# Depthwise convolution in a buffer of its own, with its taps behind each value group, its gate product read from PSUM, and the pooled maps between input chunks

## What is computed

```
mod = silu(c) @ w_ada + b_ada                    # six parts: sh1, sc1, g1, sh2, sc2, g2
h   = rmsnorm(x, norm1) * (1 + sc1) + sh1
u, gate_b, gate_c, val = split(h @ w_in)         # four times 512 columns
pooled = mean over the last 2/4/8/16 rows of u, minus u    # one window per group of 128 channels
A   = (pooled @ w_pool, per group) * pool_scale
v   = gate_c * val
B   = gate_b * (w0 * v[t-2] + w1 * v[t-1] + w2 * v[t])     # depthwise convolution, three taps
x   = x + g1 * (concat[A, B] @ w_out)
h2  = rmsnorm(x, norm2) * (1 + sc2) + sh2
x   = x + g2 * moe(h2)                           # router, top 4 of 32 experts, clamped SwiGLU
y   = rmsnorm(x, final_norm)
```

## Time and profile before

| | |
|---|---|
| median of 3 executions | 1440.04 us (1436.89 to 1440.72) |
| the profiled execution | 1436.63 us, span 1434.8 us from first to last instruction |
| granted TensorE clock, mean | 0.954 of full speed |
| busy in the span: TensorE | 1278.8 us, 89% |
| VectorE, GpSimd, ScalarE | 459.5, 282.2, 135.3 us |
| DMA | 479.23 MB, mean 334 GB/s |

### The profile page before, as it was taken

The page is one execution under the profiler, slowest core; times in us unless marked ns, Lnnn a source line. Parts: engine busy times, 40 slices in busy tenths (PEclk is TensorE's granted clock), DMA queues, the critical chain, the costliest instruction groups (busy, mean ns, idle before and its releaser), DMA issues. The chain is left out here.

```text
span 1434.8 us, 32026 instructions
## 1 busy us (share of the span) xinstructions
PE 1278.8 (89%) x13745; PEld 746.7 (52%) x13745; DVE 459.5 (32%) x676; ACT 135.3 (9%) x270; POOL 282.2 (20%) x335
## 2 busy tenths in 40 slices
PE   4999989566999999999999999999999999999710
PEld 2777634311356556655555665544545666566500
DVE  1210153452222333322223333222233333222244
ACT  3100101200000000100000000100000001000102
POOL 4002100152111111222111111221111112220126
PEclk9999989779999999999999999999999999999955
DMA  9736830625999999999999999999999999999161
GB/s 325 223 111 230 329 145 30 257 101 198 398 417 409 412 413 410 409 398 395 419 416 411 405 412 410 406 406 416 409 412 408 411 407 396 414 405 415 44 260 68
DMA packets 88787, 479.23 MB, mean 334 GB/s; under 512 B 15235, under 2 KB 24939, under 8 KB 39061
## 3 DMA queue, kind: packets, MB, share of 16 engines
q1 hardware_dynamic: 73842, 456.59, 79.5%
q0 software_dynamic: 11840, 20.64, 4.1%
q10 hardware_dynamic: 3075, 1.58, 0.5%
HBM read 468.41 MB, written 17.84 MB: 339 GB/s over the span
## 5 line engine op out<-in xcount | busy, mean ns | idle before, releaser
L1433 PE MATMUL acc<-raw_b,ht 128*32 128x512 f32 x3120 | 376.2, 597 | 16.2 <-DVE ht L1264 9.0
L1433 PE MATMUL acc<-raw,ht 128*32 128x512 f32 x3024 | 371.6, 596 | 12.5 <-DVE ht L1264 6.5
L1433 PEld LDWEIGHTS acc<-raw,ht 128*32 128x32 f32 x3024 | 168.7, 110 | 185.2 <-issue 155.4
L1433 PEld LDWEIGHTS acc<-raw_b,ht 128*32 128x32 f32 x3120 | 146.2, 110 | 220.7 <-issue 204.2
L1154 POOL DMA_INDIRECT rows<-h_rows,row_next x90 | 91.6, 1018 | 752.2 <-DVE row_next L1259 732.8
L1312 DVE TENSOR_TENSOR g_sb<-acc,bias_gu 128x768 f32<-128x768 f32 x32 | 30.7, 958 | 623.7 <-PE acc L1433 623.7
L1451 PE MATMUL acc<-raw,at 128*32 128x256 f32 x3168 | 198.2, 379 | 2.7 <-DVE at L1270 2.6
L1451 PE MATMUL acc<-raw_b,at 128*32 128x256 f32 x2976 | 186.9, 379 | 0.0
L1451 PEld LDWEIGHTS acc<-raw,at 128*32 128x32 f32 x3168 | 144.2, 109 | 37.1 <-DVE at L1270 3.1
L1451 PEld LDWEIGHTS acc<-raw_b,at 128*32 128x32 f32 x2976 | 138.2, 110 | 41.2 <-issue 8.3
L909 PE MATMUL acc<-h_t,raw 128*128 128x288 f32 (+1 forms) x512 | 118.4, 393 | 1.1 <-DVE h_t L670 1.1
(11 more groups left out here) (217 smaller groups left out, 546.1 us busy)
## 6 DMA issues: line engine op xcount, KB each, us to landing
raw<-in_w_down SPq DMA_DIRECT2D x66, 1024.0 KB, 9.0
raw_b<-in_w_gate SPq DMA_DIRECT2D x65, 1024.0 KB
raw_b<-in_w_up SPq DMA_DIRECT2D x65, 1024.0 KB
raw<-in_w_gate SPq DMA_DIRECT2D x63, 1024.0 KB, 7.0
raw<-in_w_up SPq DMA_DIRECT2D x63, 1024.0 KB, 9.3
raw_b<-in_w_down SPq DMA_DIRECT2D x62, 1024.0 KB
raw<-in_w_ada SPq DMA_DIRECT2D x24, 1024.0 KB, 11.7
raw<-in_w_in SPq DMA_DIRECT2D x8, 1024.0 KB, 13.8
```

The source lines that it names most:

```text
L1433: mm = pe.matmul(gu_ps[b][q * TB:(q + 1) * TB, :].rearrange("p (m n) -> p m n", m=2), ht[:, b, k, :], w[:, kk, :, q * CW:(q + 1) * CW], st ...
```

## The change

The convolution's result gets a tile of its own in `ring_b`, behind `g1_bc`, so that `mix_t` becomes a list of eight views: four in `h_t`, four in `conv`. The three taps of a group, prompt and sample, follow the value product of that group. The gate_b groups are not copied out by ScalarE: VectorE multiplies `conv` by them straight from PSUM, and TensorE waits for these products before it reuses the buffer. The sample's pooled windows move ahead of these products, the addition of SC2 behind the second, that of G2 behind the fourth. Three pooled maps run between `ada(SC2)` and `project(7)`, the fourth after `ada(G2)`, in other PSUM banks than before; ScalarE writes them to `h_t` once the last projection is done. On SP's queue, store(3) goes ahead of expert loads 2 to 5, and these wait for the last mix as well. "..." marks what is left out.

```diff
@@ -139,7 +139,6 @@
         junk = sb("junk", [P, D])
         h_row = [sb(f"h_row{i}", [P, D]) for i in range(2)]
         h_t = sb("h_t", [P, KT, NTOK])
-        mix_t = h_t
...
         pooled = done_first([GR, NTOK])
-        conv = h_t[:, GR:2 * GR, :]
...
         vext = done_first([GR, CPAST + SEQ])
         vext_s = done_first([GR, DEC_B, CPAST + DEC_T])
         g1_bc = done_first([D])
+
+        conv = done_first([GR, NTOK])
...
+        mix_t = [h_t[:, g, :] for g in range(GR)] + [conv[:, g, :] for g in range(GR)]
...
-        pm_p = [acc_g[:, 0, :], acc_g[:, 1, :], acc_u[:, 0, :], acc_u[:, 1, :]]
+        pm_p = [tp[:, 0, :], tp[:, 1, :], acc_y[:, 1, :], tp[:, 0, :]]
         mixp = [acc_g, acc_u]
...
@@ -355,10 +356,11 @@
                 store(t)
             sp.wait_ge(tp_full, TP["so0"] + 1)
             sp.wait_ge(new_packed, 4)
+            store(3)
             sp.wait_ge(x1_ready, PT)
+            sp.wait_ge(mix_done, TT)
             for n in range(2, SLOTS):
                 first(n)
-            store(3)
             for n in range(XSLOTS - OUT_CH, XSLOTS):
                 sp.wait_ge(*used(DENSE_CH - XSLOTS + n))
                 first(n)
...
@@ -563,17 +565,15 @@
                 leave(GR + g, gate_c[:, g, 0:SEQ], by_seq(gate_c[:, g, SEQ:NTOK]))
-            leave(3 * GR, gate_b[:, 0, 0:SEQ], by_seq(gate_b[:, 0, SEQ:NTOK]))
-            leave(3 * GR + 1, gate_b[:, 1, 0:SEQ], by_seq(gate_b[:, 1, SEQ:NTOK]))
-            leave(3 * GR + 2, gate_b[:, 2, 0:SEQ], by_seq(gate_b[:, 2, SEQ:NTOK]))
-            leave(3 * GR + 3, gate_b[:, 3, 0:SEQ], by_seq(gate_b[:, 3, SEQ:NTOK]))
 
             for g in range(GR):
                 act.wait_ge(pm_done, g + 1)
-                act.activation(mix_t[:, g, 0:SEQ], pm_p[g], ACT.Identity, scale=par[:, g:g + 1]).then_inc(pm_ready, 1)
+                if g == 0:
+                    act.wait_ge(z_done, 4 * GR)
+                act.activation(mix_t[g][:, 0:SEQ], pm_p[g], ACT.Identity, scale=par[:, g:g + 1]).then_inc(pm_ready, 1)
             act.wait_ge(tp_full, TP["pm_s"] + 1)
             for g in range(GR):
-                act.activation(mix_t[:, g, SEQ:NTOK], tp[:, 0, g * NS:(g + 1) * NS], ACT.Identity,
+                act.activation(mix_t[g][:, SEQ:NTOK], tp[:, 0, g * NS:(g + 1) * NS], ACT.Identity,
                                scale=par[:, g:g + 1]).then_inc(pm_ready, 1)
...
+            def by_seq(t_):
+                return t_.rearrange("p (s t) -> p s t", t=DEC_T)
+
+            def taps(v, y, g):
+
+                n = y.shape[-1]
+                tap = [par[:, (1 + j) * GR + g:(1 + j) * GR + g + 1] for j in range(3)]
+                step(dve.tensor_scalar(y, v[..., 0:n], tap[0], None, ALU.mult))
+                step(dve.scalar_tensor_tensor(out=y, in0=v[..., 1:1 + n], scalar=tap[1], in1=y,
+                                              op0=ALU.mult, op1=ALU.add))
+                step(dve.scalar_tensor_tensor(out=y, in0=v[..., 2:2 + n], scalar=tap[2], in1=y,
+                                              op0=ALU.mult, op1=ALU.add))
+
             add_ada(G1)
             for g in range(GR):
 
@@ -715,29 +728,11 @@
                 dve.tensor_tensor(vext_s[:, g, :, CPAST:CPAST + DEC_T], z_sample[f % 2],
                                   gate_c[:, g, SEQ:NTOK].rearrange("p (s t) -> p s t", t=DEC_T), ALU.mult)\
                     .then_inc(v_s_ready, 1)
+                dve.wait_ge(v_ready, g + 1)
+                dve.wait_ge(v_s_ready, g + 1)
+                taps(vext[:, g, :], conv[:, g, 0:SEQ], g)
+                taps(vext_s[:, g, :, :], by_seq(conv[:, g, SEQ:NTOK]), g)
             add_ada(SH2)
-            add_ada(SC2)
-            dve.wait_ge(n2_loaded, 16 * Q)
-            scale_rows(SC2, n2_rows)
-
-            def taps(v, y, b, g, ready):
-
-                n = y.shape[-1]
-                tap = [par[:, (1 + j) * GR + g:(1 + j) * GR + g + 1] for j in range(3)]
-                step(dve.tensor_scalar(y, v[..., 0:n], tap[0], None, ALU.mult))
-                step(dve.scalar_tensor_tensor(out=y, in0=v[..., 1:1 + n], scalar=tap[1], in1=y,
-                                              op0=ALU.mult, op1=ALU.add))
-                step(dve.scalar_tensor_tensor(out=y, in0=v[..., 2:2 + n], scalar=tap[2], in1=y,
-                                              op0=ALU.mult, op1=ALU.add))
-                if b is not None:
-                    dve.tensor_tensor(y, y, b, ALU.mult).then_inc(ready, 1)
-
-            add_ada(G2)
-            dve.wait_ge(z_done, 4 * GR)
-            dve.wait_ge(v_ready, GR)
-            for g in range(GR):
-                dve.wait_ge(z_evac, 2 * (2 * GR + g + 1))
-                taps(vext[:, g, :], conv[:, g, 0:SEQ], gate_b[:, g, 0:SEQ], g, conv_ready)
             bufs = [b[:, 0:DEC_B * (PAST + DEC_T)].rearrange("p (s r) -> p s r", s=DEC_B) for b in wsum]
             for g, w in enumerate(WINDOWS):
...
@@ -746,13 +741,18 @@
                                          in1=uext_s[:, g, :, PAST:PAST + DEC_T],
                                          op0=ALU.mult, op1=ALU.subtract).then_inc(pooled_s_ready, 1)
                 dve.wait_ge(pooled_s_ready, g + 1)
-            dve.wait_ge(v_s_ready, GR)
-
-            def by_seq(t_):
-                return t_.rearrange("p (s t) -> p s t", t=DEC_T)
-
             for g in range(GR):
-                taps(vext_s[:, g, :, :], by_seq(conv[:, g, SEQ:NTOK]), by_seq(gate_b[:, g, SEQ:NTOK]), g, conv_s_ready)
+                f = 3 * GR + g
+                dve.wait_ge(z_done, f + 1)
+                v = conv[:, g, 0:SEQ].rearrange("p (b n) -> p b n", b=2)
+                dve.tensor_tensor(v, v, z_prompt[f % 2], ALU.mult).then_inc(conv_ready, 1)
+                v = by_seq(conv[:, g, SEQ:NTOK])
+                dve.tensor_tensor(v, v, z_sample[f % 2], ALU.mult).then_inc(conv_s_ready, 1)
+                if g == 1:
+                    add_ada(SC2)
+                    dve.wait_ge(n2_loaded, 16 * Q)
+                    scale_rows(SC2, n2_rows)
+            add_ada(G2)
 
...
@@ -898,8 +898,11 @@
                     if 2 * GR + 2 <= f < 3 * GR + 2:
                         pe.wait_ge(v_ready, f - 2 * GR - 1)
                         pe.wait_ge(v_s_ready, f - 2 * GR - 1)
+                    elif f >= 3 * GR + 2:
+                        pe.wait_ge(conv_ready, f - 3 * GR - 1)
+                        pe.wait_ge(conv_s_ready, f - 3 * GR - 1)
                     elif f >= 2:
-                        pe.wait_ge(z_evac, 2 * (f - 1 if f < 2 * GR + 2 else f - 1 - GR))
+                        pe.wait_ge(z_evac, 2 * (f - 1))
...
             ada(SH2)
             project(6)
             ada(SC2)
+            pe.wait_ge(small_loaded, 16 * 3)
+            pe.wait_ge(pooled_ready, GR)
+
+            def pool_map(g):
+                pe.matmul(pm_p[g], wpool_sb[:, g, :], pooled[:, g, 0:SEQ], start=True, stop=True).then_inc(pm_done, 1)
+
+            for g in range(GR - 1):
+                pool_map(g)
             project(7)
             ada(G2)
-
-            pe.wait_ge(small_loaded, 16 * 3)
-            pe.wait_ge(pooled_ready, GR)
-            for g in range(GR):
-                pe.wait_ge(z_evac, 2 * (3 * GR - 1 + g // 2))
-                pe.matmul(pm_p[g], wpool_sb[:, g, :], pooled[:, g, 0:SEQ], start=True, stop=True).then_inc(pm_done, 1)
+            pe.wait_ge(pm_ready, 1)
+            pool_map(GR - 1)
 
             def mix(t):
 
                 r, out_ = norm_rows(t), mixp[t % 2]
                 if t >= 2:
                     pe.wait_ge(x1_ready, t - 1)
+                if t == 1:
+                    pe.wait_ge(conv_s_ready, GR)
                 for j in list(range(GR, 2 * GR)) + list(range(GR)):
                     w = chunk("out", j // KC)
+                    if t == 0 and j >= GR:
+                        pe.wait_ge(conv_ready, j - GR + 1 if j < 2 * GR - 2 else GR)
+                    if t == 0 and j < GR:
+                        pe.wait_ge(pm_ready, j + 1)
                     if t == PT:
                         for q in range(Q):
-                            mm = pe.matmul(out_[q * NS:(q + 1) * NS, 0, 0:QW], mix_t[:, j, SEQ:NTOK],
+                            mm = pe.matmul(out_[q * NS:(q + 1) * NS, 0, 0:QW], mix_t[j][:, SEQ:NTOK],
                                            w[:, j % KC, q * QW:(q + 1) * QW], start=(j == GR), stop=(j == GR - 1))
                         continue
                     for h in range(2):
-                        mm = pe.matmul(out_[0:r, h, :], mix_t[:, j, t * P:t * P + r],
+                        mm = pe.matmul(out_[0:r, h, :], mix_t[j][:, t * P:t * P + r],
                                        w[:, j % KC, h * HALF:(h + 1) * HALF], start=(j == GR), stop=(j == GR - 1))
                 mm.then_inc(mix_done, 1)
...
-            pe.wait_ge(pm_ready, GR)
-            pe.wait_ge(conv_ready, GR)
+
+            pe.wait_ge(conv_ready, GR - 1)
+            pe.wait_ge(conv_s_ready, GR - 1)
             mix(0)
             take("pm_s")
```

## The result

The changed kernel took 1431.28 us (median of 10 runs, 1425.69 to 1434.27), the kernel before 1439.23 us (10 runs, 1435.52 to 1443.10). The ratio is 0.9944, 95% interval 0.9927 to 0.9961: 8.1 us faster, between 5.6 and 10.5. The profiled execution took 1431.78 us with a span of 1429.7 us, 5.1 us less than before.

A forecast was written before the change was run, and what follows sets the result against it. The first block's end was taken to hang on store(4), queued behind expert loads. Mixing stage -10.2 us plus queue +5.5 gave -4.7, from 1440.0 to 1435.3 us; the range was 1429 to 1439.5.

The forecast's parts named there:

- The hole and the clock: Ahead of mix(0): closing TensorE's hole gains 7.8 us, and mix(0) without the clock drop 2.4, together 10.2 us.
- Taps, windows, gate products, maps at cost 0: Projections: moved taps and windows fit VectorE's idle time, PSUM gate products take equally long, moved maps keep TensorE's sum; cost 0.
- w_out chunks (rival C): Before mix(0): w_out chunks land late and stall it; net +2.9 us (1443) to +9.1 us (1449), chance 0.04.
- store(4) behind the loads, and the block's end behind store(4): End of first block: store(4) lands after the expert loads queued ahead, at 286.3, and the second block waits for it.
- rival A: End of first block: loads do not carry the end; gain up to 11.9 us, time 1428 to 1430, chance 0.10.
- queue term: SP's queue: it starts with store(3) at 264.69 instead of loads at 259.16, so its end shifts 5.5 us later.
- The sum: Whole kernel: -10.2 us from the mixing stage plus 5.5 from the queue gives -4.7 us, time 1435.3 us.
- the rivals: Block end free of loads, chance 0.10; new small wait and clock dip, 1438 to 1441, 0.12; late w_out chunks, 0.04.
- Faster by over 0.3%: Whole kernel: gain of more than 4.3 us; given 0.54 for faster, against 0.42 same and 0.04 slower.
- The dip of the clock: Later mixes: mix(2) took 15.68 instead of 13.98 us; without that dip the gain is 6.4, with one more 3.0.

The follow-up runs named there:

- convolution part alone: The changed kernel with conv in the tile gate_b instead of the ring and SP's queue as before the change: ratio 0.9923 to the kernel before, 10.7 us faster.
- late maps: The changed kernel with all four pooled maps after ada(G2), as before the change: ratio 0.9960 to the kernel before, 5.5 us faster.
- copied gate: The changed kernel with gate_b copied out by ScalarE and the product reading the SBUF copy: ratio 0.9955 to the kernel before, 6.5 us faster.
- queue part alone: The kernel before with only store(3) ahead of loads 2 to 5 and these waiting for the last mix: ratio 1.0037, 5.1 us slower.
- store(3) behind: The changed kernel with loads 2 to 5 ahead of store(3) again, both waits kept: ratio 0.9952 to the kernel before, 6.7 us faster.
- the repetition: The whole change, unedited, run again against the kernel before on the chip where that takes 1437.8 us: ratio 0.9940, 8.6 us faster.

## Why the prediction was right, point by point

- **The hole and the clock: 10.2 us.** Right: 10.37 in the profile, 10.7 (9.0 to 12.5) by the convolution part alone.
- **Taps, windows, gate products, maps at cost 0.** Right, each with cover left: 3 us behind the taps, 2.9 behind the windows, 3.7 between the last gate product and mix(0). The late maps and the copied gate, each undone alone, leave project(6) to mix(0) at 40.45 us. All of the gain comes from the taps' new place; of the parts in the change's title, the gate product from PSUM and the moved maps are worth nothing as long as the rest is there (both undone together wasn't run).
- **w_out chunks (rival C).** mix(0) runs 13.9 us without a gap; the late three landed in 4.7, 6.5 and 9.3 us. The last, issued at 177.68, was there at 187.0, and mix(0) comes to it at 187.11 + 3.5 = 190.6.
- **store(4) behind the loads, and the block's end behind store(4).** Right, and shown from both sides: the queue part alone costs time, and taking the store away from behind the loads brings time in both kernels. In all eight profiles in which it was queued behind them, store(4) landed 0.2 to 0.4 us after the last load (before 0.4, after 0.2, with store(3) behind 0.3). The prediction set this against the Trainium skill (DMA: Bandwidth & Descriptors, Queues, rings and completion order), by which completions need not come in order. It had read half of the rule: the same section says that the increment that reports a transfer lands only after every earlier write of the same DMA engine, so store(4) can't report ahead of loads on engines that it shares with them. With that half the rule agrees with the traces and gives rival A no ground. One reading of the prediction was slightly off: TensorE was 3.3 us ahead of store(4)'s landing (286.3 - 283.03), and the 3.9 are to the second block's start.
- **The size of the queue term** is the step that was off: "its end shifts by 264.69 - 259.16 = 5.5 us". It shifted by 3.2 (after), 3.4 (the repetition) and 3.6 (queue part alone). The same bytes needed 27.1 us from the queue's first issue to store(4)'s landing before, 24.9 after. I had taken that stretch as fixed, on the ground that the DMA engines were full in it. Rows of one microsecond show where it went:

Stretches (columns as in rows 1), the kernel before:

```profile
260.00:261.00 1.00, 1.00 (x24) 0.60 (x20) 0.00 (x0) 0.83 (x2) 0.47 (x1) 1.00 0.76 156
282.00:283.00 1.00, 0.69 (x20) 0.61 (x20) 0.20 (x1) 0.00 (x0) 0.00 (x0) 0.50 0.95 387
283.00:284.00 1.00, 0.03 (x2) 0.00 (x0) 0.00 (x0) 0.00 (x0) 0.00 (x0) 0.50 0.27 107
284.00:285.00 1.00, 0.00 (x0) 0.00 (x0) 0.00 (x0) 0.00 (x0) 0.00 (x0) 0.50 0.10 41
```

Stretches (columns as in rows 1), the changed kernel:

```profile
257.00:258.00 1.00, 0.58 (x6) 0.34 (x4) 0.86 (x4) 0.38 (x1) 0.00 (x0) 1.00 0.73 295
278.00:279.00 1.00, 0.00 (x0) 0.00 (x0) 0.00 (x0) 0.00 (x0) 0.00 (x0) 0.50 0.99 418
279.00:280.00 1.00, 0.00 (x0) 0.00 (x0) 0.00 (x0) 0.00 (x0) 0.00 (x0) 0.50 0.62 246
280.00:281.00 1.00, 0.00 (x0) 0.00 (x0) 0.00 (x0) 0.00 (x0) 0.00 (x0) 0.50 0.06 25
```

Stretches (columns as in rows 1), the kernel with store(3) behind:

```profile
279.00:280.00 1.00, 0.00 (x0) 0.00 (x0) 0.00 (x0) 0.00 (x0) 0.00 (x0) 0.50 0.90 373
280.00:281.00 1.00, 0.00 (x0) 0.00 (x0) 0.00 (x0) 0.00 (x0) 0.00 (x0) 0.50 0.17 70
```

By the busy shares the engines start at about 260.2 before and at 257.3 after, are busy until 283.0 and 279.0 (with 246 GB/s in the microsecond behind), and store(4) lands at 286.3 and 281.4. So the head is 0.2 us shorter (1.0 against 0.8), the busy stretch 1.1 (22.8 against 21.7) and the tail 0.9 (3.3 against 2.4), in which before only 107 and 41 GB/s and then less still ran. The split between stretch and tail is rough, as the share of the next microsecond is 0.62 after and 0.27 before. With store(3) put back behind four loads the stretch is 22.9 us (257.1 to 280.0), as long as before, but the tail is 2.0 (landing at 282.0). So, as far as one profile tells, store(3) in front goes with the shorter stretch, and the shorter tail has another cause. The convolution part alone, with SP's queue of before, has the long tail too (276.0 to 279.2): in these two, four loads start about 6 us ahead of the other four, and 34 KB more of state stores run in that time. Which of this matters, and how the 16 engines shared the bytes, no run shows; the cause stays open.
- **The sum.** -4.7 was forecast, the profiles give -7.2 and the runs -8.1 (-10.5 to -5.6); of the 2.5 us between the first two, 2.3 are the queue term; the rest is within the interval. The time, 1431.3, lies in the range but 4 us below the forecast: the 3.3 by which the medians' difference (8.0) is larger than 4.7, and 0.8 by which the kernel before is faster in ten runs (1439.2) than in the three that I started from (1440.0). The range had been drawn for the rivals and not for doubt in the queue term, so that it still held the time owes something to luck. "Faster by over 0.3%" held.
- The dip of the clock behaved as feared: it came in mix(2) before, in mix(3) after, with late maps in mix(4), and with store(3) behind in both mix(2) and mix(4). Before and after it costs the same (15.68 - 13.98 and 8.81 - 7.11, 1.7 us each), so it is no part of their difference.

## What to carry to other kernels

Before costing a delay on a DMA queue, find what is last at the next barrier; a small store behind a batch of prefetches can hold up every engine, and putting it in front was worth more (3.6 us in the kernel before and 6.5 in the changed one, by the distance in the profiles) than the moved maps and the gate product from PSUM, which brought nothing. When a tile is laid into a buffer that is also a prefetch slot, cost the prefetch's new start along with the instructions that the tile sets free, and ask whether the barrier can be cut loose from it. But don't push all prefetches behind the last store: here, eight loads of 1 MB put there were still running when the next stage's first small gathers came, and cost 2.7 us.

## What the runs showed of the hardware

The kernel before ran in 1386 and 1387 us on two chips and in 1438 us on a third. The whole difference is in the experts' loop and in the first gathers: from gate_up(0) to the third block's first product 1024.7 us (queue part alone) against 1072.3 (before), and 10.9 against 14.4 us from the block's start to gate_up(0). The mixing stage agrees to a few hundredths of a us (mix(0) 16.32 against 16.35, mix(1) 13.98 on both). In 400 to 1280 us the DMA engines moved 416 to 419 GB/s in the profiles of the faster chips and 407 to 410 in those of the slower, at a share of 1.01 in all. That is 2%, and the loop differs by 4.6%; what else differs no run shows. The distances in the first block carry over between them, microsecond totals less well.

The granted clock at the start of the projections was 2.4 GHz throughout in four of the twelve profiles and half of it for 3 to 10 us in the other eight, whichever the kernel. project(6) starts at 137.3 to 137.9 us in the four and at 138.8 to 141.7 in the eight, so this moves the whole execution by 1 to 4 us, and a difference of spans between two profiles can hide or feign a small gain; distances from a common instruction behind it don't, unless a second dip lies inside them. In seven of the eight TensorE had waited 0.2 to 0.8 us for a chunk of `w_ada` at about 26 us, in none of the four; the eighth, the changed kernel's, has no such wait, so this isn't the whole cause.
